# Starting the first projection on half of the contraction: modulated rows 0 to 511 first

## What is computed

```
mod = silu(c) @ w_ada[i] + b_ada[i]                    # 1024 x 6144
sh_m, sc_m, g_m, sh_f, sc_f, g_f = split(mod, 6)
h = rms_norm(x, norm_mix) * (1 + sc_m) + sh_m          # 256 x 1024
qkv = h @ w_qkv                                        # 1024 x 3072
q, k = rms_norm per head of 128;  softmax(q k^T, causal) v;  @ w_o
x = x + g_m * y;   then a gated FFN, and three more layers
```

## Time and profile before

| | us |
|---|---|
| median of 3 runs | 1393.76 |
| lowest, highest | 1391.22, 1394.17 |
| the profiled execution | 1394.08 |
| its span, first to last instruction | 1392.4 |
| TensorE busy in the span | 1325.4 (95%) |
| VectorE busy | 1041.9 (75%) |
| ScalarE busy | 762.7 (55%) |

### The profile page before, as it was taken

One profiled execution on the slowest core, in us unless ns is written; L12 is line 12 of the kernel. 1 busy time (PEld: TensorE's weight loads), 2 busy tenths in 40 slices (PEclk: granted clock), 3 DMA queues, 4 the chain that ended last, 5 costly groups with the idle time before them and its releaser, 6 DMA issues.

```text
span 1392.4 us, 19347 instructions
## 1 busy us (share of the span) xinstructions
PE 1325.4 (95%) x7398; PEld 1136.3 (82%) x7398; DVE 1041.9 (75%) x1079; ACT 762.7 (55%) x782; POOL 77.9 (6%) x81
## 2 busy tenths in 40 slices
PE   4999999999999899999999989999998989999995
PEld 4988778888899788887999978888878968888884
DVE  7887878887777674554575758899886466889997
ACT  2665543333534534433474447877765575777773
POOL 0000000000100000000000010000111200000000
PEclk9999999999899999999999999999999999999998
DMA  9997589997676475555443443999993522699991
GB/s 357 388 322 241 188 268 310 308 309 264 221 244 197 156 270 183 181 181 181 160 144 122 121 137 130 318 348 349 349 370 101 184 64 89 228 317 352 350 352 64
DMA packets 208909, 327.70 MB, mean 235 GB/s; under 512 B 9457, under 2 KB 146353, under 8 KB 208833
## 3 DMA queue, kind: packets, MB, share of 16 engines
q1 hardware_dynamic: 195536, 276.71, 59.1%
q0 software_dynamic: 13296, 49.93, 10.6%
HBM read 325.56 MB, written 1.05 MB: 235 GB/s over the span
## 4 chain that ended last, share of the span: by engine, by line
PE 84%; DVE 8%; ACT 3%; DMA 2%; issue 1%; SPq 1%; POOL 0%; DVEq 0%; ACTq 0%
PE ps L2368 24%; PE ps L2370 24%; PE ps L2369 24%; ACT w_high L718 2%; DVE w_low L1456 2%; PE ps L2904 2%; PE ps L3131 1%; PE ps L2747 1%; PE ps L3027 1%; DMA raw<-in_w_qkv 1%; PE ps L2479 1%; DVE h_low L2232 1%; DVE stats L2020 1%; DVE x_rows L2014 1%; DVE small L1581 1%
## 5 line engine op out<-in xcount | busy, mean ns | idle before, releaser
L1456 DVE TENSOR_TENSOR w_low<-raw,w_high 128x2048 fp32r<-128x2048 f32 x254 | 594.2, 2344 | 217.4 <-ACT w_high L718 215.1
L718 ACT ACTIVATE w_high<-raw 128x2048 fp32r<-128x2048 f32 x254 | 484.4, 1908 | 294.6 <-PE ps L2370 272.3
L2368 PE MATMUL ps<-w_high,h_high 128*128 128x512 f32 (+1 forms) x888 | 351.5, 396 | 8.7 <-DVE h_low L1588 4.5
L2370 PE MATMUL ps<-w_high,h_low 128*128 128x512 f32 (+1 forms) x888 | 344.5, 388 | 0.0
L2369 PE MATMUL ps<-w_low,h_high 128*128 128x512 f32 (+1 forms) x888 | 344.4, 388 | 0.0
L2368 PEld LDWEIGHTS ps<-w_high,h_high 128*128 128x128 f32 x888 | 167.8, 189 | 43.3 <-issue 6.8
L2370 PEld LDWEIGHTS ps<-w_high,h_low 128*128 128x128 f32 x888 | 167.8, 189 | 34.5
L2369 PEld LDWEIGHTS ps<-w_low,h_high 128*128 128x128 f32 x888 | 168.0, 189 | 31.6 <-issue 0.2
L2368 PE MATMUL ps<-h_high,w_high 128*128 128x256 f32 x592 | 173.1, 292 | 5.3 <-DVE h_low L1588 5.3
L2369 PE MATMUL ps<-h_low,w_high 128*128 128x256 f32 x592 | 169.1, 286 | 0.0
L2370 PE MATMUL ps<-h_high,w_low 128*128 128x256 f32 x592 | 169.0, 286 | 0.0
(11 more groups left out here) (392 smaller groups left out, 1390.3 us busy)
## 6 DMA issues: line engine op xcount, KB each, us to landing
raw<-in_w_down SPq DMA_DIRECT2D x124, 512.0 KB, 4.9
raw<-in_w_gate_up SPq DMA_DIRECT2D x88, 512.0 KB, 5.5
scratch<-in_w_ada POOLq DMA_DIRECT2D x40, 1024.0 KB, 5.6
raw<-in_w_gate SPq DMA_DIRECT2D x80, 512.0 KB, 5.0
raw<-in_w_up SPq DMA_DIRECT2D x80, 512.0 KB, 6.3
raw<-in_w_qkv SPq DMA_DIRECT2D x24, 512.0 KB, 16.7
raw<-in_w_o SPq DMA_DIRECT2D x24, 512.0 KB, 4.7
raw<-in_w_in SPq DMA_DIRECT2D x24, 512.0 KB, 5.3
```

The source lines that it names most:

```text
L718: act.activation(wh[u % SPL][:, :, 0:w], raw[u % RAW][:, :, 0:w], ACT.Copy).then_inc(h_split, 1)
L1456: dve.tensor_tensor(wl[u % SPL][:, :, 0:w], raw[u % RAW][:, :, 0:w], wh[u % SPL][:, :, 0:w].bitcast(F32), ALU.subtract).then_inc(l_split, 1)
L2368: pe.matmul(o, h1, h2, start=start, stop=False, skip_group_check=True)
L2370: return pe.matmul(o, l1, h2, start=False, stop=stop, skip_group_check=True)
```

## The change

Six things are changed. (1) SyncE loads chunk 0 and chunk 2 of `w_ada` first (halves 0, 1, 4, 5), then the first unit of query chunk 0, then halves 2 and 3, then the first unit of key chunk 2, halves 6 and 7, and the second units of both. (2) Scale and shift are formed in two halves (`half_cols`), and `h` in two halves (`half_mod`), rows 0 to 511 first; in each half VectorE makes the first group and ScalarE the second. (3) TensorE does unit 0 on the first half of `h`, then the sums and the direct products of chunk 1, then the first half of unit 1, the sums of chunk 3, the second half of unit 1, and then units 2 and 3 on the second half of `h`. Both pairs of banks are in use meanwhile. (4) `keep_busy` goes from 10 to 14 products and moves ahead of unit 0. (5) The square sums of the first queries move from between units 2 and 3 to behind unit 3. (6) On VectorE the key norm and the masks come between the two parts of `ada(0, 5)`, ahead of the splits of units 6 and 7, and the second part follows those splits. The other edits shift counters.

```
# SyncE
-            for h in range(2, 6):
-                first_ada(h)
-            for h in range(6, 8):
-                sp.wait_ge(ada_used, h - 5)
-                first_ada(h)
+            first_ada(4)
+            first_ada(5)
...
-            for c in (0, 2, 1, 3, 4, 5):
+            columns(A["w_qkv"][0], 0, NC, (0,))
+            first_ada(2)
+            first_ada(3)
+            columns(A["w_qkv"][0], 2 * NC, NC, (0,))
+            for h in (6, 7):
+                sp.wait_ge(ada_used, h - 5)
+                first_ada(h)
+            columns(A["w_qkv"][0], 0, NC, (UK,))
+            columns(A["w_qkv"][0], 2 * NC, NC, (UK,))
+            for c in (1, 3, 4, 5):
# ScalarE
+            def half_mod(q):
+                scale, shift = mod(0)
+                g = 2 * q + 1
+                act.wait_ge(mod_taken, q + 1)
+                if q == 0:
+                    act.wait_ge(xt_ready, xt.up(4))
+                for j in range(2):
+                    k, b = 2 * g + j, ps[:, 4 + g, j * S:(j + 1) * S]
+                    act.activation(b, b, ACT.Identity, bias=shift[:, k:k + 1], scale=scale[:, k:k + 1]).then_inc(act_step, 1)
+                    step.up()
+                act.wait_ge(v_ready, v.up())
+                act.activation(hh[:, 4 * q:4 * q + 2, :], shifted_parts(q), ACT.Copy).then_inc(hh_ready, 1)
+                hhr.up()
+                act.wait_ge(act_step, step.value())
+                act.activation(hh[:, 2 * g:2 * g + 2, :], bank_k(g), ACT.Copy).then_inc(hh_ready, 1)
+                hhr.up()
             ahead(-2)
-            transposed_mod(*mod(0), 1)
+            half_mod(0)
             ahead(0)
+            half_mod(1)
...
-            ahead(PLAN["qkv"] + 1)
+            ahead(PLAN["qkv"] + 2)
             qk_out(0)
# VectorE
+            def half_cols(q, bank):
+                dve.wait_ge(mod_sums, msum.up())
...                                    # the three operations of mod_cols, on four columns of eight
+            def half_mod(q, between=None):
+                scale, shift = mod(0)
+                g = 2 * q
+                if q == 0:
+                    dve.wait_ge(xt_ready, xt.up(4))
+                for j in range(2):
+                    k = 2 * g + j
+                    i = dve.tensor_scalar(shifted_parts(q)[:, j, :], ps[:, 4 + g, j * S:(j + 1) * S],
+                                          scale[:, k:k + 1], shift[:, k:k + 1], ALU.mult, ALU.add)
+                i.then_inc(v_ready, 1)
+                dve.wait_ge(v_ready, v.up())
+                if between:
+                    between()
+                dve.wait_ge(hh_ready, hhr.up())
+                dve.tensor_tensor(hl[:, 2 * g:2 * g + 2, :], shifted_parts(q), hh[:, 2 * g:2 * g + 2, :].bitcast(F32),
+                                  ALU.subtract).then_inc(h_ready, 1)
+                hr.up()
+                low(g + 1)
-            for h in (0, 1, 2):
-                first_ada(h)
+            first_ada(0)
+            first_ada(1)
             rms_apply()
-            for h in (4, 5, 6, 7):
-                first_ada(h)
-            ahead(-2)
-            mod_cols(0, 0, 3)
-            transposed_mod(*mod(0))
+            first_ada(4)
+            first_ada(5)
+            half_cols(0, 3)
+            half_mod(0, lambda: ahead(-2))
+            first_ada(2)
+            ahead(-1)
+            first_ada(6)
+            first_ada(7)
             ahead(0)
+            half_cols(1, 4)
+            half_mod(1)
...
             qk_norm(0)
-            ada(0, 5, acc_of(0, 5))
-            ahead(PLAN["qkv"] + 5)
+            ada(0, 5, acc_of(0, 5), parts=(0,))
             qk_norm(1)
             masks()
+            ahead(PLAN["qkv"] + 5)
+            ada(0, 5, acc_of(0, 5), parts=(1,))
             maxima(MOBA, EARLY_BANKS, 0)
# TensorE
+            def half_unit(pair, q, blocks, fresh=False):
...                                    # the given blocks of a unit: 12 products each
             first_sums(0)
-            first_direct(1)
-            pe.wait_ge(ada_used, usedd.up())
-            first_sums(1)
             pe.wait_ge(xn_ready, xn.up())
-            transposes(tv)
+            transposes(tv, range(4))
             pe.wait_ge(ada_used, usedd.up(2))
-            first_sums(2)
+            first_sums(2).then_inc(mod_sums, 1)
+            msum.up()
+            keep_busy(14, 0)
+            pe.wait_ge(mod_taken, mtk.up())
+            half_unit(0, 0, (0, 1, 2, 3), fresh=True)
+            pe.wait_ge(ada_used, usedd.up())
+            first_sums(1)
+            first_direct(1)
+            half_unit(2, 0, (0, 1))
             pe.wait_ge(ada_used, usedd.up(2))
             first_sums(3).then_inc(mod_sums, 1)
             msum.up()
-            keep_busy(10, 0)
+            half_unit(2, 0, (2, 3))
             pe.wait_ge(mod_taken, mtk.up())
+            half_unit(0, 1, (0, 1, 2, 3), fresh=True)
+            half_unit(2, 1, (0, 1, 2, 3))
...
-            chunk("features", fresh=True)
-            chunk("features", between=lambda: head_sums(0))
+            head_sums(0)
             chunk("features", between=lambda: head_sums(1))
```

More of the change, by code:

```diff
@@ L895, in qk_out @@
                 b = 4 * (0, 2, 1, 3)[c]
-                act.wait_ge(unit_used, PLAN["qkv"] + 2 * c + 2)
+                act.wait_ge(unit_used, PLAN["qkv"] + (3 if c == 0 else 2 * c + 2))
                 act.activation(FT[:, b:b + 4, :].rearrange("p k t -> p (k t)"),
@@ L966, in _ @@
             wo("wo0")
-            norm_first(1, 3)
+            norm_first(1, 4)
             silr, atr, ahr = Count(sil_ready), Count(at_ready), Count(ah_ready)
@@ L1024, in _ @@
             root_table()
-            norm_first(0, 5)
+            norm_first(0, 6)
             ahead(PLAN["win"])
@@ L1054, in _ @@
             wo("wout")
-            norm_first(1, 7)
+            norm_first(1, 8)
             ffn("ffn1", NFF, True)
@@ L1604, in first_ada @@
                     w, s = first_halves[h][:, k, :], scol[:, UK * (h % 2) + k:UK * (h % 2) + k + 1]
-                    if k == 0 and h in (0, 2, 4, 6):
+                    if k == 0 and h % 2 == 0:
                         i = dve.tensor_scalar(acc, w, s, None, ALU.mult)
@@ L1610, in first_ada @@
                     dve.wait_ge(ada_used if k == UK - 1 else ada_acc, (usedd if k == UK - 1 else accd).up())
-            for h in (0, 1, 2):
-                first_ada(h)
-            rms_apply()
-            for h in (4, 5, 6, 7):
-                first_ada(h)
-            ahead(-2)
-            mod_cols(0, 0, 3)
-            transposed_mod(*mod(0))
+            def half_cols(q, bank):
+                dve.wait_ge(mod_sums, msum.up())
+                o, o1 = slice(4 * q, 4 * q + 4), slice(8 + 4 * q, 12 + 4 * q)
+                m, b, gain = ps[:, bank, 0:16], cols[:, C_BADA:C_BADA + 16], cols[:, C_NMIX:C_NMIX + 8]
+                dve.tensor_tensor(modB[:, o], m[:, o], b[:, o], ALU.add).then_inc(dve_step, 1)
+                dve.wait_ge(dve_step, step.up())
+                dve.tensor_tensor(modA[:, o], m[:, o1], b[:, o1], ALU.add).then_inc(dve_step, 1)
+                dve.wait_ge(dve_step, step.up())
+                dve.scalar_tensor_tensor(modA[:, o], modA[:, o], 1.0, gain[:, o], ALU.add, ALU.mult).then_inc(mod_taken, 1)
+                dve.wait_ge(mod_taken, mtk.up())
@@ L2492, in first_cols @@
             def first_cols(c, q, first):
-                return ps[:, 3, 4 * c + q:4 * c + q + 1], dict(start=first, stop=False, skip_group_check=True)
+                return ps[:, 4 if c % 2 else 3, 4 * c + q:4 * c + q + 1], dict(start=first, stop=False, skip_group_check=True)
             def first_sums(c):
                 for q in range(4):
-                    o, flags = first_cols(c, q, c == q == 0)
+                    o, flags = first_cols(c, q, c < 2 and q == 0)
                     i = pe.matmul(o, acc_of(0, c)[:, q * P:(q + 1) * P], ones[:, 0:1], **flags)
@@ L2511, in first_direct @@
                 return i
+            def half_unit(pair, q, blocks, fresh=False):
+                if blocks[0] == 0:
+                    pe.wait_ge(l_split, lsp.up())
+                for b in blocks:
+                    o = ps[:, pair + b // 2, (b % 2) * S:(b % 2 + 1) * S]
+                    for k in range(UK):
+                        bank_of_h(fresh and b == 0, k)
+                        cs = slice(b * P, (b + 1) * P)
+                        i = mm3(o, wh[n[0] % SPL][:, k, cs], wl[n[0] % SPL][:, k, cs], hh[:, UK * q + k, :], hl[:, UK * q + k, :],
+                                q == k == 0 and b % 2 == 0, q == 1 and k == UK - 1)
+                if blocks[-1] == UK - 1:
+                    i.then_inc(unit_used, 1)
+                    used.up()
+                    n[0] += 1
+                    lin[0] += q
             pe.wait_ge(small_loaded, 32)
@@ L2515, in _ @@
             first_sums(0)
-            first_direct(1)
+            pe.wait_ge(xn_ready, xn.up())
+            transposes(tv, range(4))
```

(9 more changed lines are left out.)

## The result

Over 20 runs of each on one chip the changed kernel takes 1397.95 (1393.76 to 1400.40), the kernel before 1392.86 (1389.99 to 1396.13); compared run by run the ratio is 1.0033, 95% interval 1.0023 to 1.0043: 4.6 slower. The forecast was 1398.5. The profiled execution took 1399.91 (before 1394.08), its span is 1398.0 (1392.4); these two lie 2.0 and 1.2 above the medians of their kernels, so the profiles differ by 5.6 to 5.8 where the runs differ by 4.6.

The account below looks back on a forecast made before the run. TensorE was taken to bound the kernel (84% of the chain), with VectorE's order deciding whether it waits. Head start -1.4, hold +4.5 and clock +1.7 gave +4.8, so 1398.5; range 1392.0 to 1400.5, the forecast's own 1396.5 to 1400.5.

Parts of the forecast that it names:

- Start of unit 0: Opening: TensorE starts the projection at 28.6 instead of 39.1, a head start of 10.5.
- `keep_busy`: Ahead of unit 0: fourteen products, at the rate of ten in 4.11, end near 28.5 and stay hidden.
- Direct products: After unit 0 and the sums of chunk 1: about 5.3, bounds 3.6 and 7.0, the clock falling in their course.
- First half of unit 1: Behind the direct products: 2.9 plus 1.6 for the slow clock, to 45.3.
- Head start left at unit 5: Unit 5 starts at 70.2, before at 71.65: 1.4 left; 4.4 with full clock, 0.5 if the clock returns a window later.
- Hold at the turn: After unit 6, TensorE waits 4.5 for the scaled exponentials because of VectorE's new order; overlaps and a late split give 4.2 to 5.0.
- Clock behind the hold: Behind the turn: TensorE's idling brings the clock down and costs 1.7 more, bounds 0 and 1.7.
- (a): Opening: the clock stays full through the contraction, head start 4.4, in all +1.8, 1395.5; chance 0.22.
- (b): Turn between units 6 and 7: head start outlives the hold, no hold or cold clock, 1389.4 to 1392.4; chance 0.12.
- (c): At the turn: the hold comes but the clock does not fall behind it, +3.1, 1396.9; chance 0.10.
- (d): Unit 3, 6 or 7: a load or split counted as just in time is late as well, +7, 1401; chance 0.06.
- (e): Opening: half 5 or unit 0 lands as late as before, so TensorE gains 5 less; chance 0.02.

Follow-up runs that it names:

- the two with the part moved: Changed kernel with the second part of `ada(0, 5)` behind probs(0): with splits of units 6 and 7 back ahead of the norm 1394.97, with nothing else moved 1392.72.
- the shifted parts: Changed kernel with the second part of `ada(0, 5)` behind probs(0) and later parts of chunks 6 to 8 one meeting later each: 1393.12, 0.9994 against the kernel before.
- The one-part experiment: Changed kernel with only the second part of `ada(0, 5)` moved behind probs(0): 1392.72, 1.0004 against the kernel before.
- the order alone: Kernel before with only VectorE's new order (key norm and masks ahead of the splits of units 6 and 7, second part of `ada(0, 5)` behind them): 1399.16, 1.0041.
- moved part: Changed kernel, second part of `ada(0, 5)` behind probs(0), splits of units 6 and 7 back ahead of the norm: 1394.97, 1.0009 against the kernel before.

## Why the prediction was right, step by step

The sign and the mechanism of the loss held: a small head start, a hold at the turn because work stands ahead of the maxima in VectorE's list, and a fall of the clock behind it. The time came out within 0.6 of the forecast, and that closeness is partly luck. In the profiled pair the change costs 5.6 to 5.8, by the ratio of the runs 4.6, and the two profiled executions of the changed kernel end 2.6 apart by stretches of half clock that the change does not touch.

- **Start of unit 0**: 28.6 forecast, 29.71 measured in both profiles of the changed kernel. There the sums of chunk 2, 1.05 forecast from the earlier trace rows, ran at the slow rate and took 1.86 (22.94); the remaining 0.3 lies on the path through VectorE and in the `keep_busy` products. In three other kernels with the same opening (the two with the part moved, and the shifted parts) the same sums took 1.05 and unit 0 started at 28.50 to 28.69, as forecast. So this term varies between executions and was not wrong for all of them.
- **`keep_busy`**: forecast to end near 28.5. By the rate that the forecast names, fourteen products take 5.75 and end at 29.65, so this sum was wrong. Measured are 5.0 to 5.3, and they end with the low part of `h`, so that the slip cost at most some 0.1 to 0.2.
- **Direct products**: 5.3 forecast, 4.5 measured (36.36 to 40.84). The clock fell in their course, as forecast, but about 2.5 in, so that more of them were fast.
- **First half of unit 1**: 4.5 forecast, 5.1 measured. The clock came back later than the price taken from before the FFN said. Unit 2: 49.3 forecast, 50.13.
- **Head start left at unit 5**: 1.4 forecast, 0.46 measured, below the bound of 0.5; 1.5 to 1.7 in the three executions in which the sums of chunk 2 ran fast (square sums at 68.21 to 68.44). The sign that was named for it, square sums 1 to 2 earlier, failed in both profiles of the changed kernel.
- **Hold at the turn**: 4.5 forecast; turn less square sums grew by 4.52 (4.06 + 0.46), of which 3.93 is the wait itself and 0.25 the wait for the split of unit 6; 0.3 is not traced. The one-part experiment and the order alone show it by taking away and adding its cause.
- **Clock behind the hold**: 1.7 forecast, 1.70 measured (5.76 - 4.06).
- **Sum**: +4.8 forecast; -0.46 + 4.52 + 1.70 = +5.8 in the profiles, +4.6 by the ratio of the runs. The profiles miss the forecast by the head start. That the runs do not is what one expects if part of the executions have the larger head start, but only the profiled ones can be looked into.

The rivals: (a), the clock full through the contraction, is out by the windows at 39 and 43. The Trainium skill, "TensorE: Matmul & The Clock Gate", Part 1, has the clock follow how busy TensorE has been; read with weight loads as busy, that gave this rival, and the trace does not agree with that reading (busy 1.00, clock 0.50). The sum of rival (a) has a slip: with `h` at 46.0, unit 5 would start at 66.9 and not 67.2; nothing else hangs on it. (b), the head start outliving the hold, is out by the wait; with the part alone moved away most of the gain is spent at the second turn, and with the later parts shifted as well 1.3 of it reach the FFN, too little for the runs to resolve. (c), no fall behind the hold, is out by the window at 91. (d) is there only as 0.25 at unit 6; it becomes real, as 1.2, when TensorE is 4.5 earlier still. (e), a late half 5 or unit 0, is out by the start at 29.71.

## What to carry to other kernels

When a start is moved forward, first list what lay in the dead time that it closes: most of these 9.4 went to sums and direct products that used to be free and to the slow clock that they brought. On an engine with a strict list, work that nobody needs soon must not stand between two instructions of a round trip: one part of 3.1 cost 4 to 5.6 by the ratios, and the clock behind the hold made a hold of 3.9 into 5.6. A gain upstream reaches the end only if each later meeting has slack for it; here the load of `ada(0, 5)`, the split of unit 6 and the second turn each took some back. And a difference of 1 or 2 in 1400 cannot be read from one pair of profiles: look at where it arises, and take its size from many runs.

## What the runs showed of the hardware

- Among the direct products, ten wide records after every eight did not keep the clock: it fell at 38.1 and stayed at 0.50 for 13.7, where without them it was 6.8 in six profiles.
- Without any direct products it fell as well, at 41.3 for 3.4, behind the wait of 1.75 for chunk 3.
- The stretches at 0.50 inside these programs last 3.4, 6.8, 10.2 (before, near 358) or 13.7 (moved part, at 157.1). Which comes in a place varies between executions of one program: near 830 the changed kernel has 6.8 once and 3.4 once. A stretch of 6.8 and the wait beside it moved one kernel by 2.7, as much as the gain looked for.
- Eight one-column records took 0.95 in some places and 1.86 in others with the clock column at 1.00 (22.94 lies before the first fall that the profile shows): the rate of the records says more than the column there. The sums of chunk 2 took 1.86 in some executions and 1.05 in others of kernels with the same opening, and unit 0 starts 0.6 to 1.2 later with the slow ones.
